# Recurrent mixer: the triangular inverse's products for both heads at once, and side work moved

## The reference

```python
def step(state, inp):
    r_t, w_t, k_t, v_t, a_t, b_t = inp
    sa = jnp.einsum('bhvk,bhk->bhv', state, a_t)
    state = state * w_t[:, :, None, :] + sa[..., None] * b_t[:, :, None, :] + v_t[..., None] * k_t[:, :, None, :]
    y = jnp.einsum('bhvk,bhk->bhv', state, r_t)
    return state, y
```

## Time and profile before

| | us |
|---|---|
| median of 3 runs | 2857.4 (2849.94 to 2857.96) |
| the profiled execution | 2856.87 |
| its span in the profile | 2855.0 |
| busy in the span: TensorE, VectorE, ScalarE, GpSimd | 2743.1, 1465.4, 1268.8, 1127.8 |

### The profile page before, as it was taken

One profiled execution on the slowest core, in us unless ns is written; L12 is line 12 of the kernel. 1 busy time (PEld: TensorE's weight loads), 2 busy tenths in 40 slices (PEclk: granted clock), 3 DMA queues, 4 the chain that ended last, 5 costly groups with the idle time before them and its releaser, 6 DMA issues.

```text
span 2855.0 us, 54997 instructions
## 1 busy us (share of the span) xinstructions
PE 2743.1 (96%) x23332; PEld 2187.8 (77%) x23332; DVE 1465.4 (51%) x2561; ACT 1268.8 (44%) x2296; POOL 1127.8 (40%) x634
## 2 busy tenths in 40 slices
PE   7899999979999999999999999999999999999999
PEld 5568888857778888877888876577777777788887
DVE  7865886057757777753888303612222224344410
ACT  5664443233556555644444225534444454422221
POOL 4124444534543332314444454034333443544443
PEclk9999999999999999999999999999999999999999
DMA  5102332322300000012233232023221332333232
GB/s 164 49 31 90 95 96 90 95 96 82 102 23 6 7 8 7 6 46 71 92 96 94 88 99 66 23 89 98 75 75 52 96 96 74 96 96 96 88 95 77
DMA packets 63460, 208.88 MB, mean 73 GB/s; under 512 B 11248, under 2 KB 11504, under 8 KB 62832
## 3 DMA queue, kind: packets, MB, share of 16 engines
q1 hardware_dynamic: 60704, 193.10, 21.9%
q0 software_dynamic: 1936, 10.91, 1.1%
q10 hardware_dynamic: 576, 1.35, 0.1%
HBM read 199.95 MB, written 4.19 MB: 72 GB/s over the span
## 4 chain that ended last, share of the span: by engine, by line
PE 86%; DVE 9%; ACT 2%; issue 2%; POOL 1%; DMA 0%; SPq 0%; DVEq 0%; ACTq 0%
PE banks L1658 21%; PE banks L1660 21%; PE banks L1659 21%; PE banks L779 9%; PE banks L1800 1%; DVE low L539 1%; PE banks L830 1%; DVE arena L2641 1%; PE banks L772 1%; PE banks L856 1%; PE banks L1776 1%; PE banks L1695 1%; PE banks L861 1%; PE banks L872 1%; PE banks L1848 1%
## 5 line engine op out<-in xcount | busy, mean ns | idle before, releaser
L312 POOL TENSOR_TENSOR low<-arena,high 128x1024 fp32r<-128x1024 f32 (+1 forms) x376 | 876.7, 2332 | 1328.8 <-ACT high L303 1328.7
L1658 PE MATMUL banks<-high,high 128*128 128x512 f32 (+1 forms) x2752 | 1093.4, 397 | 40.9 <-POOL low L312 24.1
L1660 PE MATMUL banks<-high,low 128*128 128x512 f32 (+1 forms) x2752 | 1082.3, 393 | 0.0
L1659 PE MATMUL banks<-low,high 128*128 128x512 f32 (+1 forms) x2752 | 1082.3, 393 | 0.0
L303 ACT ACTIVATE high<-arena 128x1024 fp32r<-128x1024 f32 (+1 forms) x376 | 381.9, 1016 | 800.9 <-PE banks L1660 799.5
L1658 PEld LDWEIGHTS banks<-high,high 128*128 128x128 f32 x2752 | 519.9, 189 | 171.6 <-POOL low L312 18.0
L1660 PEld LDWEIGHTS banks<-high,low 128*128 128x128 f32 x2752 | 519.9, 189 | 120.7
L1659 PEld LDWEIGHTS banks<-low,high 128*128 128x128 f32 x2752 | 520.2, 189 | 118.6 <-issue 1.9
L779 PE MATMUL banks<-arena 64*64 64x64 f32 x7680 | 291.5, 222 | 9.7 <-DVE arena L1544 3.4
L779 PEld LDWEIGHTS banks<-arena 64*64 64x64 f32 x7680 | 251.2, 135 | 58.1 <-issue 23.8
L2538 DVE TENSOR_TENSOR arena<-banks,arena 128x512 f32<-128x512 f32 x48 | 33.1, 691 | 425.1 <-PE banks L1660 423.9
(11 more groups left out here) (292 smaller groups left out, 2915.9 us busy)
## 6 DMA issues: line engine op xcount, KB each, us to landing
arena<-weights SPq DMA_DIRECT2D x302, 512.0 KB, 3.5
arena<-weights SPq DMA_DIRECT2D x48, 448.0 KB, 3.2
arena<-weights SPq DMA_DIRECT2D x28, 256.0 KB, 2.6
arena<-tables POOLq DMA_DIRECT2D x5, 448.0 KB, 3.6
arena<-x_t SPq DMA_DIRECT2D x4, 512.0 KB, 5.8
x_spill<-arena POOLq DMA_DIRECT2D x1, 2048.0 KB, 9.3
arena<-small_weights POOLq DMA_DIRECT2D x16, 128.0 KB, 2.6
arena<-x_spill POOLq DMA_DIRECT2D x1, 2048.0 KB, 9.3
```

Of the source, the lines that this page charges most:

```text
L312: pool.tensor_tensor(lo[:, 0:n], ring[w % RING][:, 0:n], hi[:, 0:n].bitcast(F32), ALU.subtract).then_inc(w_low, 1)
L1658: pe.matmul(dst, hi[:, c], x[0], start=kt == 0, stop=False)
L1659: pe.matmul(dst, hi[:, c], x[1], start=False, stop=False)
L1660: mm = pe.matmul(dst, lo[:, c], x[0], start=False, stop=kt == kts_of[t] - 1)
```

## The change

`both_heads` issues the products of both heads in one go: for each q and p first head 0, then head 1, and head 1 writes to the other half of the partitions (`p ^ h`). Two such products in a row bring head 1 back to its own half. `square` 1 and 2, the first `grow`, both `merge`s and the last two `grow`s use it; `square` 3 and `grow` 3 and 4 stay by head. The copies of S1, S2, Q1 and Q2 and the adds U2, U5 and U6 become one operation for both heads, and so do the three mask operations. GpSimd makes one matrix more, UX: head 1's start matrix in exchanged halves. The waits that were by head become one.

`exclusive` moves on VectorE from behind the round's last add (slot U6) to slot U5. In the first round a ScalarE table load moves ahead of S1, a hidden copy behind T, and on GpSimd `k_sum` ahead of the low parts; one weight split moves from round 0 to round 4. Outside the mixer: the last `sines` moves into the attention's fourth pair, the four bias operations go behind the splits of the `a_k` tiles, and the c branch's fill is cut 3+1 k-tiles around the last head sum in place of 4 behind it.

```diff
+        def both_heads(into, col, lhs, rhs):
+            last = [None, None]
+            for q in range(2):
+                for p in range(2):
+                    for h in range(2):
+                        last[h] = pe.matmul(into[h][hf(p ^ h), col + C * q:col + C * q + C], lhs(hf(p), h, q), rhs(hf(p), h, q),
+                                            start=True, stop=True)
+            return last
...
-        def square(i, h, s):
+        def square(i, s):
             if s == 1:
-                d2.wait(pe, i, f"D_{h}")
+                d2.wait(pe, i, "D")
...
+            both_heads(PJ, 0, mt, m)
+            mm = both_heads(PJ, P, m, mt)
+            for h in range(2):
+                p2.inc(mm[h], f"S{s}_{h}")
...
+        def first_grow(i):
+            d2.wait(pe, i, "M")
+            g2.wait(pe, i, "U1_1")
+            mm = both_heads(PI, 0, halves_of(R.P2, 1), lambda r, h, q: R.UX[r, q, :] if h else R.U[i % 2][r, 0, q, :])
...
+        def late_grow(i, m):
+            a2.wait(pe, i, f"Q{m}")
+            mm = both_heads(PI, 0, halves_of(R.P2, 1), halves_of(R.P2, 0))
...
-                for s in (2, 3):
-                    for h in range(2):
-                        square(i, h, s)
-                        grow(i, h, s)
+                square(i, 2)
+                first_grow(i)
+                for h in range(2):
+                    last_square(i, h)
+                    grow(i, h, 3)
...
+            def both(name, dst):
+                p2.wait(act, i, f"{name}_1")
+                a2.inc(act.activation(dst.rearrange("p h k b -> p h (k b)"), both_j[:, :, 0:256], ACT.Copy), name)
...
-                for h in range(2):
-                    ev("S2", h, flat(R.P4[:, h, :, :]), 256)
-                if i == 0:
-                    act.preload_act_table_set("natural_log_exp_and_others")
-                    act.activation(R.h_high[1], R.a1h, ACT.Copy).then_inc(h_high, 1)
+                both("S2", R.P4)
...
-                d2.wait(pool, i, f"D_{h}")
+                d2.wait(pool, i, "D")
+                if h:
+                    g2.wait(pool, i, "U1_0")
+                    for p in range(2):
+                        u_ = pool.tensor_tensor(R.UX[hf(1 - p), :, :], R.D[hf(p), 1, :, :],
+                                                eye[hf(p), :].unsqueeze(1).to_broadcast([C, 2, C]), ALU.add)
...
+            if c == 0:
+                k_sum(j)
             if i == 0:
                 hidden_low(0)
                 second_low(1)
                 hidden_low(1)
-            if c == 0:
-                k_sum(j)
-            if i == 0:
+            if i == TT:
                 advance_tiles(tiles_of["rw_g1"][0:1])
...
             elif at_ == (1, "U5") and more:
                 centre(j + 1, 0)
-            elif at_ == (1, "U6") and more:
                 exclusive(j + 1, 0)
...
+            def add_both(s):
+                p2.wait(dve, i, f"U{s}_1")
+                u = R.U[i % 2].rearrange("p h q c -> p h (q c)")
+                d2.inc(dve.tensor_tensor(u, both_i[:, :, 0:P], u, ALU.add), f"U{s}")
...
-        for h in range(4):
+        advance("a_q")
+        for h, t in enumerate(tiles_of["a_k"]):
+            advance_tiles([t])
             pool.tensor_scalar(B.biasA[:, h, :], B.dist, -SLOPE_A[h], None, ALU.mult).then_inc(bias_ready, 1)
-        advance("a_q", "a_k", "a_v")
+        advance("a_v")
...
-            sines(last)
             value(1)
+            return lambda: sines(last)
```

More of the change, by code:

```diff
@@ L756, in scores @@
             if i:
-                a2.wait(pe, i - 1, "Q2_1")
+                a2.wait(pe, i - 1, "Q2")
             for q in range(2):
@@ L765, in scores @@
             if i:
-                d2.wait(pe, i - 1, "U6_1")
+                d2.wait(pe, i - 1, "U6")
             for k in range(2):
@@ L798, in square, with last_square @@
-            p2.inc(mm, f"S{s}_{h}")
+                d2.wait(pe, i, "D")
+                m, mt = (lambda r, h, q: R.D[r, h, q, :]), halves_of(R.NM, 0)
+            else:
+                a2.wait(pe, i, "S1")
+                m, mt = halves_of(R.P2, 0), halves_of(R.P2, 1)
+            both_heads(PJ, 0, mt, m)
+            mm = both_heads(PJ, P, m, mt)
+            for h in range(2):
+                p2.inc(mm[h], f"S{s}_{h}")
+        def last_square(i, h):
+            a2.wait(pe, i, "S2")
+            p2.inc(product(PJ[h], 0, half_of(R.P4, h, 0), half_of(R.P4, h, 1)), f"S3_{h}")
@@ L808, in grow @@
                 lhs = half_of(R.P4, h, 1)
-            elif s == 4:
+            else:
                 d2.wait(pe, i, f"U3_{h}")
                 lhs = lambda r, q: R.D[r, h, q, :]
-            else:
-                a2.wait(pe, i, f"Q{s - 4}_{h}")
-                lhs, u = half_of(R.P2, h, 1), half_of(R.P2, h, 0)
             p2.inc(product(PI[h], 0, lhs, u), f"U{s}_{h}")
-        def merge(i, h, m):
-            u = lambda r, q: R.U[i % 2][r, h, q, :]
-            if m == 1:
[L820 to L823, removed]
+        def late_grow(i, m):
+            a2.wait(pe, i, f"Q{m}")
+            mm = both_heads(PI, 0, halves_of(R.P2, 1), halves_of(R.P2, 0))
+            for h in range(2):
+                p2.inc(mm[h], f"U{m + 4}_{h}")
@@ L825, in tokens, with merge @@
+        def merge(i, m):
+            u = lambda r, h, q: R.U[i % 2][r, h, q, :]
+            if m == 1:
+                a2.wait(pe, i, "T_1")
+            d2.wait(pe, i, "U4_1" if m == 1 else "U5")
+            both_heads(PJ, 0, halves_of(R.NM, m), u)
+            mm = both_heads(PJ, P, u, lambda r, h, q: eye[r, :])
+            for h in range(2):
+                p2.inc(mm[h], f"Q{m}_{h}")
         def tokens(i, h):
@@ L851, in solve @@
             c, st = it % TT, 2 * it + q
-            d2.wait(pe, it, "U6_1")
+            d2.wait(pe, it, "U6")
             dc.wait(pe, st, "X")
@@ L924, in pe_rwkv @@
                 aux(i, 0)
-                square(i, 0, 1)
-                square(i, 1, 1)
+                square(i, 1)
             if seq:
@@ L947, in pe_rwkv @@
                 aux(i, 1)
-                for h in range(2):
-                    merge(i, h, 1)
-                for h in range(2):
-                    grow(i, h, 5)
+                merge(i, 1)
+                late_grow(i, 1)
                 aux_gate(i)
@@ L955, in pe_rwkv @@
             if off:
[L956 to L959, removed]
+                merge(i, 2)
+                late_grow(i, 2)
                 aux_left(i, 1)
@@ L1122, in act_rwkv @@
                     ksq(j + 1)
+                if i == 0:
+                    act.preload_act_table_set("natural_log_exp_and_others")
                 if c == 1 and more:
@@ L1128, in act_rwkv @@
                     shifted_bonus(j - 1, PP[1])
-                for h in range(2):
-                    ev("S1", h, flat(R.P2[:, h, :, :]), 256)
+                both("S1", R.P2)
                 if i == 0:
@@ L1166, in act_rwkv @@
                     factor(j + 1, "F")
-                for h in range(2):
-                    ev("Q1", h, flat(R.P2[:, h, :, :]), 256)
+                both("Q1", R.P2)
                 if c == 0 and more:
@@ L1175, in act_rwkv @@
             if off:
-                for h in range(2):
-                    ev("Q2", h, flat(R.P2[:, h, :, :]), 256)
+                both("Q2", R.P2)
                 if c == 2 and j:
@@ L1491, in spread @@
                     centre(j + 1, 1)
+                    exclusive(j + 1, 1)
                 if j >= 2:
                     z_gate(j - 2, PP[1])
-            elif at_ == (2, "U6") and more:
-                exclusive(j + 1, 1)
             elif at_ == (3, "M") and more:
@@ L1547, in dve_rwkv @@
             if off:
-                for h in range(2):
-                    d2.inc(dve.tensor_tensor(R.AM[i % 2][:, h, :, :], four[h][:, :, C:4 * C], lanes, ALU.mult), f"M_{h}")
+                d2.inc(dve.tensor_tensor(R.AM[i % 2], four[:, :, :, C:4 * C], lanes.unsqueeze(1).to_broadcast([P, 2, 2, 3 * C]),
+                                         ALU.mult), "M")
                 spread(i, "M")
-                add_u(2)
+                add_both(2)
                 spread(i, "U2")
```

65 lines of the change are left out of this document (30 added, 35 removed).

## The result

| | us, median | runs | range | TensorE's mean granted clock, median of the runs |
|---|---|---|---|---|
| before | 2851.9 | 12 | 2847.2 to 2858.0 | 0.992 (in the 64 runs that stand beside the experiments) |
| changed | 2859.3 | 12 | 2848.2 to 2871.3 | 0.9865 |

The ratio is 1.0031, with a 95% interval of 1.0019 to 1.0043: slower by a little, where faster by 0.35% was forecast. (The forecast of 2847 counted from the 2857.4 of three runs; twelve runs put the kernel before at 2851.9.) The changed kernel also scatters over 23 us, and its time follows the clock: the fastest run, 2848.2, had 0.991, the slowest, 2871.3, 0.983, and the twelve lie near a line of 2.4 us per 0.001. The profiled execution took 2857.28 us, span 2855.5.

What follows compares the result with a forecast made beforehand. It took TensorE to bound the kernel (96% busy, 86% of the chain), with waits absorbing its savings. Rounds +1, first round -3.2, bias -4.6 and local attention -3.1 gave -9.9, so 2847 us, range 2824 to 2872.

Steps and rivals of the forecast that it cites:

- Its chain: Recurrent rounds: waits for in-flight products, copies and adds stay, so almost none of TensorE's saved issue time shortens a round.
- rival D: Recurrent rounds: new TensorE idle lowers the clock in one round in ten, 24 us, 2871; chance 0.06.
- Pace, copies, adds, links: Two-head blocks: records 15 to 16 ns apart, copy 0.59, add 0.42, merge 1 to merge 2 2.42 us.
- the other side of the bound: Pace of `both_heads` products: bounded by 15 ns below and 29 ns above, the latter no gain in pace.
- rival C: Two-head products: neighbours sharing rows don't overlap, 72 us over 32 rounds, 2919; at 20 ns 2874; chance 0.10.
- The offer of 79 us: Recurrent stage: 176 records a round moved to four quadrants, 2.5 us less issue a round; almost none expected as gain.
- Sum of the rounds, +1: Recurrent stage: changes of links, `exclusive` and gate rounds over all rounds add to +1 us, in effect nothing.
- the moved `exclusive`: Seven rounds before a group's fourth: the gain becomes a new wait on ScalarE, net +0.15 each, 1.1 us together.
- gate rounds: Six rounds with two gate products between late_grow and merge 2: less issue counts there, -0.24 each, -1.4 together.
- GpSimd, "hidden": Start matrices on GpSimd: four operations in a row, 2.0 us against some 2.3 until first_grow asks, so no cost.
- Stalls: Three single waits removed: first round -3.2, bias -4.6, local attention -3.1 us.
- the wait at 805: Before, first recurrent round: TensorE's wait of 2.58 us, around which the clock fell to 0.81 in 804 to 808.

Runs made afterwards that it cites:

- e5: Changed kernel with head 1's products kept on its own half, rows p to columns p, so two quadrants: 2921.0 us, ratio 1.0244.
- e6: e3 with GpSimd's last weight split one round later, behind round 29's start matrices: 2843.2 us, ratio 0.9971.
- e11: e10 with `exclusive` in slot U5 instead of U6: 2834.5 us, ratio 0.9946.
- e10: e2 with GpSimd's last weight split behind round 29's start matrices: 2836.7 us, ratio 0.9948.
- e3: Changed kernel with an unread 256-column matmul added behind each of the two merges: 2844.7 us, ratio 0.9972.
- e7: e4 with gate products behind merge 2 in gate rounds and an unread matmul there in the others: 2841.7 us, ratio 0.9968.
- e9: e7 with GpSimd's last weight split behind round 29's start matrices: 2837.8 us, ratio 0.9956.
- e1: Kernel before with only the edits outside the mixer (last sines, biases, c fill): 2842.6 us, ratio 0.9968.
- e2: Kernel before with the edits outside the mixer and the first round's moves, heads still by themselves: 2837.8 us, ratio 0.9950.
- e8: Changed kernel with an unread 256-column matmul added behind merge 1 only: 2844.9 us, ratio 0.9984.
- e12: e3 with the added matmuls cut to 16 columns from 256: 2861.0 us, ratio 1.0030.
- e4: Changed kernel with the second piece of side work, `aux(i, 1)`, moved from ahead of merge 1 to behind it: 2854.2 us, ratio 0.9999.

## Why the prediction was wrong

Its chain was right within a few us, and the rival D, given 0.06, decided the direction.

- **Pace, copies, adds, links**: right, each link within 0.05 us, and 15 ns a record; e5 shows the other side of the bound: 72.8 us more in rounds 1 to 30 against the 72 of rival C. That its time, 2921.0, also meets C's 2919 is partly luck, since C counted from 2847 and without any fall of the clock. By the start times in the trace the gain lies where rows are shared: in square 1 at 912.03 four records, the two calls on the same rows, start 7 ns apart each, and then 38 ns pass, where `product` before (990.82) has two records and then 52. The offer of 79 us did vanish into the links.
- **Sum of the rounds, +1**: e6, in whose profile no round was hit by a fall of the clock and GpSimd is out of the way, has rounds 1 to 30 2.8 us longer than before. Mostly c = 1 (+0.25), c = 0 (+0.09) and the c = 2 rounds without a gate (+0.2). c = 3 was to lose 0.15 by the moved `exclusive` and lost 0.02; five gate rounds gained 0.11 each instead of 0.24, and the sixth, round 30, lost 0.52. Why c = 1 lost stays open; `exclusive` is not the reason, since these rounds take 14.47 by head with it moved (e11) as without (e10).
- **GpSimd, "hidden"**: right in the ordinary rounds, wrong in round 29, where a split of 2.35 us uses up the cover (a wait of 0.48 stands in two others, at 840 and 1257). It is 4 us between the profiles of e3 and e6, the clock that fell beside that wait and a longer halt of TensorE included, and 3.4 to 4 by the times of e7 and e9. The timeline of before had the split at 1232.42 ahead of the start matrices, and I had read only ordinary rounds.
- **Stalls**: first round -2.96 (said -3.2), bias -4.51 (-4.6), local attention -4.46 at the start of the recurrent stage (-3.1), a figure that varies by 3.7 us between profiles of the same code, so what the two moved operations cost there isn't settled. e1 lies at its expectation; e2 gained 14.3 us by the ratio, where the three stalls were forecast at 10.9 together.
- **The clock**: this step failed. I set the new idle time at 2.2 us a round, put it in four pieces (the two behind the merges measured 0.74, not 0.4 to 0.6), and then argued that the clock would hold since the longest piece is a third of the wait at 805. That compared the length of one wait with another, when what changed was that a round now holds four waits, with little but them behind the second merge. The price was also set wrongly: one round in ten, three falls, at 8 us each, 24 us. In the profile the clock fell eight times, and a fall costs 1.1 to 1.5 us where it meets the mask products. By the medians all of them together cost some 15 us: 14.6 by e3, 14.4 by e8, and 16.3 from e12 to e3. The profiles of the changed kernel and of e3 account for 8.9 us in rounds 0 to 30; they differ by 4.0 more outside these rounds, where their code is the same for all but the last round, so that part isn't traced to the falls in the rounds. The sign that the prediction had set for D, a clock under 0.95 in the rounds, was not met either: the stage has 0.97. It was too coarse, for in 4 us around a fall the clock is 0.57. With the clock mostly held, the change from before is -8.0 us (e3), where -10.4 was forecast. That the number 2847 stands only 2 us from e3's 2844.7 is luck, since it counted from 2857.4.

The Trainium skill, "TensorE: Matmul & The Clock Gate", has a section "A second HAM failure mode: psum-queue depth-cycling", by which frequent short idle pieces of TensorE let its clock go back and forth. The runs agree: eight stretches at the lower level in the stage of the changed kernel, five in e12, two in e3. On the row-group rule of the same page's Part 3, weighed in the prediction, the measurement decides against: in `both_heads` every second call has the rows of the call before it, its loads start 7 ns behind that call's, and the pace is 15 ns.

## What to carry to other kernels

Where an edit makes TensorE faster but not what it waits for, the gain turns into waits, and the granted clock is part of their price: look at the clock by stretches, and try the same kernel with useless work in the waits before giving the edit up or keeping it. A scatter of times that follows the mean clock is the sign. And what is called hidden in a loop of 32 rounds has to be checked in the odd rounds at both ends, where other work stands in the same queue.

## What the hardware showed unexpectedly

- With waits of 0.74 us behind both merges the clock falls, with one of them covered by added work it mostly holds (e8), with work only moved into it it doesn't (e4); 128 records more on TensorE in 32 rounds made a kernel 14.6 us faster, and the same instructions with 16 columns didn't.
- Two 64x64 products that share rows and differ in columns start within 20 ns, four records 7 ns apart; the next rows follow 38 ns later. Over a block that is 15 ns a record on four quadrants; on two it is 29 to 30, whether neighbouring calls change rows and columns together (before) or keep both for two calls (e5).
- A VectorE add of 128 columns in SBUF beside a GpSimd operation of 1.27 us took 1.32 instead of 0.29 (mean 378 ns after, 322 before, over 56 in each):

```profile
826.02 1.32 DVE L1565 TENSOR_TENSOR arena<-arena 128x128 f32<-128x128 f32 x1
```

- TensorE stood still once or twice in each of nine of the fourteen profiles, for 0.4 to 1.4 us between 1215 and 1233, waiting for nothing that the profile shows ("issue"). It is small and unexplained.
